# A third of the second feed-forward block's low parts by ScalarE and an accumulating transfer instead of VectorE

## What is computed

```python
h = rmsnorm_2(x, norm_ffn[i])
up = dwconv3(h @ ffn_w_up[i], ffn_conv_w[i], ffn_conv_b[i])
gate, val = jnp.split(up, 2, axis=-1)
x = x + (jax.nn.silu(gate) * val) @ ffn_w_down[i]
return rmsnorm_2(x, norm_final)
```

## Time and profile before

| | |
|---|---|
| time, median of 3 runs | 2552.14 us (2551.93 to 2552.97) |
| the profiled execution | 2553.46 us |
| its span, first to last instruction | 2551.6 us |
| TensorE busy | 2541.6 us |
| VectorE busy | 2120.8 us |
| ScalarE busy | 1528.2 us |
| GpSimd busy | 293.9 us |
| transfers, share of 16 engines in SyncE's queue | 59.5%, 490.80 MB |
| granted TensorE clock, mean | 0.999 |

### The profile page before, as it was taken

One profiled execution on the slowest core, in us unless ns is written; L12 is line 12 of the kernel. 1 busy time (PEld: TensorE's weight loads), 2 busy tenths in 40 slices (PEclk: granted clock), 3 DMA queues, 4 the chain that ended last, 5 costly groups with the idle time before them and its releaser, 6 DMA issues.

```text
span 2551.6 us, 36018 instructions
## 1 busy us (share of the span) xinstructions
PE 2541.6 (100%) x13720; PEld 2188.6 (86%) x13720; DVE 2120.8 (83%) x3103; ACT 1528.2 (60%) x2200; POOL 293.9 (12%) x232
## 2 busy tenths in 40 slices
PE   9999999999999999999999999999999999999998
PEld 8888888888889888888888888888888888888887
DVE  7787777777977888888888888887888888888887
ACT  6666658776656555555555566445665656555565
POOL 2111102316201000000000022101100101010101
PEclk9999999999999999999999999999999999999999
DMA  7565566566655556666566656556655656575654
GB/s 248 183 218 188 190 198 196 175 208 197 203 182 178 190 187 199 198 200 200 200 199 198 197 174 223 157 167 197 198 191 177 209 171 218 165 224 166 223 182 163
DMA packets 137349, 493.63 MB, mean 193 GB/s; under 512 B 15447, under 2 KB 16344, under 8 KB 136792
## 3 DMA queue, kind: packets, MB, share of 16 engines
q1 hardware_dynamic: 136600, 490.80, 59.5%
q10 hardware_dynamic: 576, 0.53, 0.1%
HBM read 489.14 MB, written 2.13 MB: 193 GB/s over the span
## 4 chain that ended last, share of the span: by engine, by line
PE 99%; DMA 0%; ACT 0%; DVE 0%; issue 0%; ACTq 0%
PE ps L1283 42%; PE ps L1280 21%; PE ps L1191 6%; PE ps L1192 6%; PE ps L1193 6%; PE ps L1255 5%; PE ps L1253 5%; PE ps L1254 5%; PE ps L1297 1%; PE ps L1433 0%; PE ps L1268 0%; PE ps L1269 0%; PE ps L1270 0%; PE ps L1525 0%; PE ps L1238 0%; PE ps L1237 0%
## 5 line engine op out<-in xcount | busy, mean ns | idle before, releaser
L1959 DVE TENSOR_TENSOR wl<-raw,wh 128x1024 fp32r<-128x1024 f32 (+2 forms) x798 | 969.6, 1226 | 239.5 <-ACT wh L1550 234.6
L1550 ACT ACTIVATE wh<-raw 128x1024 fp32r<-128x1024 f32 (+2 forms) x798 | 815.6, 1030 | 490.3 <-PE ps L1280 260.9
L1283 PE MATMUL ps<-X,wh 128*128 128x512 f32 x3016 | 1009.6, 395 | 1.4 <-DVE X L1965 0.7
L1280 PE MATMUL ps<-X,wl 128*128 128x256 f32 x3016 | 754.1, 278 | 0.0
L1283 PEld LDWEIGHTS ps<-X,wh 128*128 128x128 f32 x3016 | 545.5, 188 | 106.3 <-issue 3.3
L1280 PEld LDWEIGHTS ps<-X,wl 128*128 128x128 f32 x3016 | 553.6, 188 | 27.8
L1283 PE MATMUL ps<-XG,wh 128*128 128x512 f32 x896 | 298.2, 395 | 0.0
L1280 PE MATMUL ps<-XG,wl 128*128 128x256 f32 x896 | 222.2, 278 | 0.0
L1283 PE MATMUL ps<-X,XM 128*128 128x512 f32 x584 | 197.3, 394 | 0.0
L1283 PEld LDWEIGHTS ps<-XG,wh 128*128 128x128 f32 x896 | 161.1, 188 | 30.6 <-issue 0.9
L1550 ACT ACTIVATE T<-ps 128x256 f32<-128x256 f32 (+1 forms) x301 | 100.6, 384 | 135.3 <-PE ps L1280 134.7
(11 more groups left out here) (290 smaller groups left out, 3760.5 us busy)
## 6 DMA issues: line engine op xcount, KB each, us to landing
raw<-in_w_gu SPq DMA_DIRECT2D x144, 512.0 KB, 4.1
raw<-in_w_gate SPq DMA_DIRECT2D x104, 512.0 KB, 4.0
raw<-in_w_sc SPq DMA_DIRECT2D x95, 512.0 KB, 4.1
raw<-in_w_val SPq DMA_DIRECT2D x88, 512.0 KB, 3.7
raw<-in_w_zx SPq DMA_DIRECT2D x80, 512.0 KB, 3.6
raw<-in_w_downp SPq DMA_DIRECT2D x72, 512.0 KB, 4.6
raw<-in_w_down SPq DMA_DIRECT2D x60, 512.0 KB, 3.5
raw<-in_w_in SPq DMA_DIRECT2D x56, 512.0 KB, 3.6
```

The source lines that it names most:

```text
L1280: t = e.matmul(bank(c, i)[:, 0:256], held(wl, u)[:, b0:b0 + 128], X[:, kx * 512:kx * 512 + 256], start=False, stop=sp and kk == c.kn - 1)
L1283: e.matmul(bank(c, i)[:, :], held(wh, u)[:, b0:b0 + 128], X[:, kx * 512:kx * 512 + 512], start=st and kk == 0, stop=False)
L1550: return e.activation(out, in_, ACT.Copy, scale=scale)
L1959: return e.tensor_tensor(out, a, b, op)
```

## The change

`ADDED` lists 70 units: of the plain ones from unit 720 to 985 those whose number leaves 1 when divided by 3. For such a unit ScalarE writes, ahead of the rounded copy, a second copy with the factor -1 into the low part's place (semaphore `neg`). GpSimd waits for it, and for its own transfer but one (two semaphores `d_lo`), and issues a transfer that reads the unit's raw data from DRAM a second time and adds it to what stands there. VectorE leaves the subtraction of these units out. TensorE waits for the rounded copy and the transfer in place of `lo`, and SyncE takes the raw slot as free when the rounded copy is made. The piece `dadd` moves from GpSimd to VectorE. Some semaphores are shared with earlier uses, with counts shifted, to make room.

```diff
+ADDED = [u for u in range(NU) if part(u) in (None, "C") and U_DEEP + 8 <= u < NU - 12 and u % 3 == 1]
...
+def subtracted(u):
+
+    return halves(u) - len([k for k in ADDED if k <= u])
+
+
+def low_part(w, hi, lo, d_lo, u):
+
+
+    if u in ADDED:
+        k = ADDED.index(u)
+        w.wait_ge(hi, halves(u))
+        w.wait_ge(d_lo[k % 2], 16 * (k // 2 + 1))
+    else:
+        w.wait_ge(lo, subtracted(u))
...
-                w.wait_ge(lo, halves(u))
+                if u in ADDED:
+                    w.wait_ge(hi, halves(u))
+                else:
+                    w.wait_ge(lo, subtracted(u))
...
-            w.wait_ge(lo, halves(u))
+            low_part(w, hi, lo, d_lo, u)
...
-                w.wait_ge(lo, halves(u))
+                low_part(w, hi, lo, d_lo, u)
...
+                    if i in ADDED:
+                        copy(parted(wl, i), source(i), -1.0).then_inc(neg, 1)
                     copy(parted(wh, i), source(i)).then_inc(hi, 1)
...
-                if piece == "split":
+                if piece == "split" and i not in ADDED:
                     w.wait_ge(hi, halves(i))
                     tt(parted(wl, i), source(i), parted(wh, i).bitcast(F32), ALU.subtract).then_inc(lo, 1)
...
+                if piece == "dadd":
+                    w.wait_ge(htA, 4)
+                    for n, buf, q, st in ((5, dU, 0, 0), (6, dW, 0, 1), (7, dV, 1, 0), (8, dX, 1, 1)):
+                        w.wait_ge(gD, dD0(i) + n)
+                        if i.i:
+                            w.wait_ge(dG, DG + 4 * i.i)
+                        tt(hp(q, st), hp(q, st), buf, ALU.add).then_inc(dG, 1)
...
+                if piece == "split" and i in ADDED:
+                    k, (what, a, b) = ADDED.index(i), LOADS[SLOT[i]]
+                    w.wait_ge(neg, NEG + k + 1)
+                    if k > 1:
+                        w.wait_ge(d_lo[k % 2], 16 * (k // 2))
+                    e.dma_start(parted(wl, i), T_[what][a, b].bitcast(F32R), accum_op=ALU.add).then_inc(d_lo[k % 2], 16)
...
-                if piece == "dadd":
-                    w.wait_ge(htA, 4)
-                    for n, buf, q, st in ((5, dU, 0, 0), (6, dW, 0, 1), (7, dV, 1, 0), (8, dX, 1, 1)):
-                        w.wait_ge(gD, dD0(i) + n)
-                        if i.i:
-                            w.wait_ge(dG, DG + 4 * i.i)
-                        add(hp(q, st), hp(q, st), buf).then_inc(dG, 1)
```

More of the change, by code:

```diff
@@ L756, in program @@
     pV, pP, p2V = (sem(n) for n in ("pV", "pP", "p2V"))
-    htP, htA, og, outA, outV = (sem(n) for n in ("htP", "htA", "og", "outA", "outV"))
+    htP, htA, og = (sem(n) for n in ("htP", "htA", "og"))
+    d_lo = [sem(f"d_lo{i}") for i in range(2)]
+    neg, NEG, outA, outV, OUTA, OUTV = tsq, 2, dtA, dtV, 6, 13
     tS, gE, gD, gT, sbA, sbV, dG = ex, sm, dv, qk, pt, ptc, acc2
@@ L1129, in sync @@
                         e.dma_start(dst, T_[name]).then_inc(d_b2, 16)
-        for st, waits, a, b in ((0, ((outA, 2),), 0, 2), (0, ((outV, 2),), 2, 4), (1, ((outV, 3),), 2, 3), (1, ((outA, 3),), 0, 1),
-                                (1, ((outV, 4),), 3, 4)):
+        for st, waits, a, b in ((0, ((outA, OUTA + 2),), 0, 2), (0, ((outV, OUTV + 2),), 2, 4), (1, ((outV, OUTV + 3),), 2, 3),
+                                (1, ((outA, OUTA + 3),), 0, 1),
+                                (1, ((outV, OUTV + 4),), 3, 4)):
             for done, n in waits:
@@ L1688, in scalar @@
                             copy(Xf[:, 2048 * st + 512 * q:2048 * st + 512 * q + 512], hp(q, st), ocol(14, st)).then_inc(outA, 1)
-                    w.wait_ge(outA, 4)
+                    w.wait_ge(outA, OUTA + 4)
                     e.dma_start(T_["out"][:, 2560:3072], Xf[:, 2560:3072]).then_inc(d_out[2], 16)
@@ L1986, in vector @@
                     else:
-                        w.wait_ge(lo, halves([u for u in NTH if NTH[u] == q - 1][2]))
+                        w.wait_ge(lo, subtracted([u for u in NTH if NTH[u] == q - 1][2]))
                         w.wait_ge(tS, TS + 3 * q)
@@ L1996, in vector @@
                     if q:
-                        w.wait_ge(lo, halves([u for u in NTH if NTH[u] == q - 1][3]))
+                        w.wait_ge(lo, subtracted([u for u in NTH if NTH[u] == q - 1][3]))
                     tt(Td[:, 0:512], raw[:, r:r + 512], Tc[:, 0:512], ALU.add).then_inc(tS, 1)
```

## The result

| | before | after |
|---|---|---|
| median of the runs on the same chip | 2552.47 us (6 runs, 2551.49 to 2554.75) | 2561.47 us (6 runs, 2559.83 to 2565.51) |
| the profiled execution | 2553.46 us | 2561.39 us |
| its span | 2551.6 us | 2559.5 us |

The ratio is 1.0037, with a 95% interval of 1.0027 to 1.0047: 9.0 us or 0.35% slower, by the 0.2% bound a loss. The time lies in the range that was given (2550 to 2600), but not by its likeliest case, 2554.6: it is near the 2563 of the first rival, the accumulate that comes late behind the groups.

What follows compares the result with a forecast made beforehand. TensorE, busy 2541.6 of 2551.6 us, was taken as the bound. Group 0 +1.6, groups 1 to 3 +0.9 for jitter, the rest 0: +2.5 us on the median 2552.14 gave 2554.6 us, range 2550 to 2600.

Steps and rivals of the forecast that it cites:

- its likeliest case: Whole kernel: no measurable change, 2554.6 us, own range 2551 to 2557, chance 0.55.
- the first rival: Behind groups 0 to 3: accumulate lands after 10 us, 2.7 us late each, 10.7 in all, 2563 us; chance 0.29.
- What bounds the kernel: Whole kernel: TensorE runs back to back, so VectorE's net 72.8 us less is worth nothing at the end.
- The lead: First unit behind each multiplication group: from copy's start to TensorE's read, 8.7 us, in group 0 9.5.
- the new path: For a taken unit: negated copy, GpSimd's issue, accumulating transfer, TensorE; 1.03 + 0.33 + 7 = 8.4 us.
- the upper row: Landing of a plain load of twice the bytes, 8.2 us, taken as upper bound for the accumulating transfer.
- just in time: First unit behind groups 1 to 3: path of 8.4 us against a lead of 8.7, cost 0.
- Its second part: In the first rival, behind the groups: the third unit's load is 3.3 - 1.6 = 1.7 us late, overlapping the 2.7.
- Group 0's term: Behind group 0: the accumulate delays a load sharing its engines, so the 0.69 us wait grows by 1.6 us.
- The plain stretches: Steady stretches away from group ends: path of 11.2 us hidden in 16.6, transfer share rising to 0.8 to 0.95.
- The second rival: Steady stretches: transfer engines fill up; two loads' worth just fits, three costs 102 us, 2654 us; chance 0.12.
- the test of the forecast: Whole kernel: TensorE's waits stay under 6 us, those there are stand on the first unit behind a group.

Runs made afterwards that it cites:

- experiment 2: The changed kernel with only the first unit behind each of groups 0 to 3 taken (4 transfers): 2563.30 us, ratio 1.0040 to before.
- experiment 3: The changed kernel with its 70 transfers only copying, not adding, so the low part is left out of the result: 2554.40 us, ratio 1.0007 to before.
- experiment 4: The changed kernel with no unit taken, only the groups' sums moved from GpSimd to VectorE: 2552.60 us, ratio 1.0002 to before.
- experiment 7: The changed kernel with every second unit taken in place of every third (104 transfers): 2566.86 us, ratio 1.0052 to before.
- experiment 5: The changed kernel with units leaving 2 when divided by 3 (68 transfers), some inside the groups: 2578.90 us, ratio 1.0101 to before.
- experiment 6: The changed kernel with units divisible by 3 taken (70 transfers), some inside the groups: 2564.60 us, ratio 1.0047 to before.

## Why the prediction was right in range and wrong in its likeliest case

**What bounds the kernel** held: TensorE's 2541.6 us did not move, and 78.3 us less on VectorE brought nothing (predicted 72.8; the subtractions that are left run shorter, 1.18 us in the mean for 1.24; the prediction named this return and left it out of its 72.8, and why not all of it shows wasn't traced). The sums took 0.683 us each, predicted 0.681. ScalarE's union grew by 57.0 us where 72 was predicted: the 70 copies are as long as said, 1.06 us each, but neighbouring copies overlap, two in a row taking 1.99 us; why it is not 67 then was not traced.

**The lead** was right: 8.7 us predicted for group 1, 8.85 measured, and the place, the first unit behind groups 0 to 3, too. Group 0's 9.5 was too much, 8.84 measured: it ran to TensorE's start behind the old 0.69 us wait.

**The step that failed** is the size of the new path: "I take 7 us, nearer to the upper row, because the transfer reads two streams and writes one, and 0.33 us for the issue". Together 7.33 us; measured are 9.4 from the issue's start to landing, and 0.3 us between copy and issue which the sum didn't have. 1.03 + 7.33 = 8.4 us against 8.7 was "just in time"; 10.9 against 8.85 is 2.0 us late, and so in all four places, by 1.7 to 2.1. The 7 us lie near the shortest landing that after shows into `wl`, 6.7, and below their median of 8.0. The upper row, 8.2 us for a 1 MB load, was no upper bound: more bytes in a plain load are not the same as an accumulate beside the loads that follow a group. Experiment 2 shows that the other accumulates are not what makes it long (9.4 us behind group 1 with and without them), experiment 3 that the accumulation is (9.4 us against 6.0); how much of the rest the loads beside it make was not isolated.

The first rival went wrong in the other direction by little: 10 us landing, 2.7 us late, four times, 10.7 us; measured 9.4, 2.0 and 8.2. Its second part, the third unit's load coming later, did not happen.

**Group 0's term** (+1.6 us, as the load that VectorE's first sum waits for would share its engines with the accumulate) was wrong. ScalarE got that load's data at 1973.92 us, earlier than the 1975.55 before by more than the 0.9 us by which TensorE was free earlier, and the old 0.69 us wait is gone; experiment 4 shows the same without any transfer.

The delay by sharing is there and is larger than the 1.6 us taken, but it fell on the next load. Behind group 1 the fourth unit's load, issued 0.5 us behind the accumulate, landed in 8.7 us where it took 4.5 before, and the three loads behind it in 9.7, 8.9 and 7.9 where it was 5.3, 5.3 and 4.2. Experiment 2, with this one accumulate alone, has the same landings within 0.3 us; experiment 4, without any, has 5.1 at most in this stretch. So accumulate and loads are long in the same stretch. What each does to the other isn't separated, since the raw slots that come free earlier also bring the next load closer (0.3 us behind it, 1.1 before). ScalarE waits for that load:

```profile
2111.44 1.06 ACT L1573 ACTIVATE wl<-raw 128x1024 fp32r<-128x1024 f32 x1 [4.77 <-DMA raw<-in_w_gate]
```

This is the fourth unit behind group 1, so its own path begins late; its accumulate landed 0.5 us before TensorE, itself 2 us late by then, came to it (issued at 2112.79, due at 2111.86 + 8.33 = 2120.19, landed in 6.9 us).

**The plain stretches** went as forecast: share 0.95 to 0.96 (forecast 0.8 to 0.95), no wait of TensorE, matmuls unchanged. The second rival's price, about two loads' worth, was right at 2.10; its consequence, waits at every third unit once the engines are full, is refuted by experiment 7 with 104 transfers at 1.04.

That TensorE's waits would "stay under 6 us" was the test of the forecast, and it failed; "four waits of TensorE of 2 us or more ... ended by a transfer on GpSimd's queue" was the first rival's, and three came at 2.0 to 2.1 us and one at 1.72. The time lies in the wide range only because that took the first rival in, which had a chance of 0.29; the case with 0.55 failed.

## What to carry to other kernels

A step that is put ahead of a consumer is to be priced against the smallest lead in the program, here right behind stretches in which the consumer eats the buffers up, and in the crowd that is there at that moment; four late transfers of 70 made nearly all of the loss. A guess that comes out "just in time" by 0.3 us, on a duration that no row shows, is no forecast of no change: the far bound should carry more weight than the middle. And when one part of a change costs, list the units with the least lead and leave those out, before giving up the rest; but where the relieved engine doesn't bound the kernel, even the repaired change gains nothing.

## What the runs showed of the hardware that was not expected

**A wait can cost more than itself.** In experiment 2 the waits are 7.8 us and the median grew by 11.2. Its windows around group 1's end, columns as above:

```profile
2100.00:2110.00 10.00, 10.00 (x46) 8.28 (x45) 7.13 (x7) 6.15 (x7) 0.87 (x1) 1.00 0.82 229
2110.00:2115.00 5.00, 2.98 (x10) 2.20 (x9) 1.94 (x3) 2.60 (x3) 0.00 (x0) 0.75 0.79 300
2115.00:2125.00 10.00, 10.00 (x57) 8.77 (x57) 10.00 (x13) 4.82 (x5) 0.00 (x0) 0.95 0.77 247
```

Around 2.02 us without work the granted clock is 0.75 as a mean of 5 us, and it is back within the next 10. In experiment 5 it shows in TensorE's timeline behind group 0's wait:

```profile
1976.21 0.77 PE L1214 MATMUL ps<-wh,XG 128*128 128x512 f32 x1 [3.61 <-DMA wl<-in_w_downg]
1976.78 0.63 PE L1215 MATMUL ps<-wl,XG 128*128 128x512 f32 x1
1977.21 0.63 PE L1216 MATMUL ps<-wh,XG 128*128 128x512 f32 x1
1977.63 0.63 PE L1214 MATMUL ps<-wh,XG 128*128 128x512 f32 x1
```

Behind a wait of 3.61 us the 512-column matmuls follow each other every 0.43 us in place of 0.2267, the lower of the clock's two levels (1.2 GHz, not 2.4), until about 1982 us: the first 14 intervals take 6.10 us where 3.17 is usual, so 2.9 us are lost beside the wait itself. It doesn't come each time. The waits of 1.72 to 2.13 us in the profile of after left the granted clock at 1.00, and so did those of experiment 2 behind groups 0, 2 and 3. The length of the wait alone doesn't decide: in experiment 6 one of 2.43 us lowered the clock to 0.69 as a mean of 5 us, one of 2.50 us left it at 1.00.

This is a part of why the medians in the ladder lie above the waits. In the profiled executions what the waits leave of the longer span is longer busy time of TensorE: 2544.1 us in experiment 2 and 2551.3 in experiment 5, 2.5 and 9.7 more than before. With the waits for transfers, and less the old 0.69, that is 9.6 and 25.2 of the 9.7 and 25.4 us by which their spans grew. In experiment 5 the clock was low behind all four waits (0.50 to 0.79 as means of the 4 to 8 us behind them). The 2.5 us are not far above what differs anyway: experiment 4, without any such wait, is busy 1.9 us less than before. What the clock took from the other executions isn't shown, since only the profiled ones can be looked into.

**A transfer share above 1 starved nobody.** 1.04 at 302 to 304 GB/s (experiment 7) went with raw loads that land in 7.9 us in place of 6.2 to 6.3 and with no wait in the plain stretches.

**An accumulating transfer costs more than its bytes.** One of 512 KB from DRAM took 0.862 us of GpSimd's queue and 2.10 loads' worth of the engines; the same transfer without the addition 0.530 us and 1.16.
